# Mixture-of-experts weight loads: the sync engine's loop written out, and each load held until the third load before it has landed

## The reference, cut to what matters

```python
def expert_block(args):
    xb, e = args
    hid = jax.nn.silu(xb @ w1[e]) * (xb @ w3[e])   # w1[e], w3[e]: 1024 x 512
    return hid @ w2[e]                             # w2[e]: 512 x 1024
...
y_assign = y_slots[dest].astype(jnp.float32) * s_gate[:, None]
return jax.ops.segment_sum(y_assign, s_tok, num_segments=T)
```

## Time and profile before

| | |
|---|---|
| median of 3 runs | 3673.42 us (3670.94 to 3673.61) |
| the profiled execution: its own time | 3671.4 us |
| the profiled execution: span of its records | 3669.6 us, 29297 instructions |
| mean granted TensorE clock | 0.908 |
| PE busy / PEld busy | 81% / 43% |
| DVE / ACT / POOL busy | 18% / 13% / 7% |
| HBM traffic over the span | 160 GB/s |
| loads of `in_moe_w` | 192 of 2048 KB, median 24.4 us from issue to landing |
| writes of `y_slots` by ACT | 32 of 256 KB |

### The profile page before, as it was taken

One profiled execution on the slowest core, in us unless ns is written; L12 is line 12 of the kernel. 1 busy time (PEld: TensorE's weight loads), 2 busy tenths in 40 slices (PEclk: granted clock), 3 DMA queues, 4 the chain that ended last, 5 costly groups with the idle time before them and its releaser, 6 DMA issues. The chain is left out here.

```text
span 3669.6 us, 29297 instructions
## 1 busy us (share of the span) xinstructions
PE 2984.2 (81%) x12116; PEld 1559.9 (43%) x12116; DVE 673.6 (18%) x1777; ACT 489.9 (13%) x954; POOL 254.9 (7%) x247
## 2 busy tenths in 40 slices
PE   6999999999865455454455449999999999999999
PEld 4666666544642122122122126444444464444443
DVE  1222222210130000100100032332220123321102
ACT  1222232210010000000000021310000113110000
POOL 1000002210000000000000030020000110110000
PEclk9999999999977777787777679899999998999999
DMA  6211111112179998898889841112221211122220
GB/s 199 52 35 52 35 35 52 46 46 92 55 302 428 379 381 345 378 393 358 378 365 393 355 174 71 58 46 69 80 92 69 71 60 68 41 74 80 78 83 35
DMA packets 192664, 587.39 MB, mean 160 GB/s; under 512 B 16434, under 2 KB 142642, under 8 KB 167730
## 3 DMA queue, kind: packets, MB, share of 16 engines
q1 hardware_dynamic: 186210, 569.19, 40.3%
q10 hardware_dynamic: 4160, 8.39, 0.6%
q0 software_dynamic: 2192, 8.39, 0.6%
HBM read 571.26 MB, written 14.68 MB: 160 GB/s over the span
## 5 line engine op out<-in xcount | busy, mean ns | idle before, releaser
L2310 PE MATMUL bank<-arena 128*128 128x512 f32 (+2 forms) x1472 | 608.9, 576 | 9.1 <-DVE arena L1675 9.1
L1068 PE MATMUL bank<-arena 128*32 128x512 f32 x2048 | 264.5, 674 | 224.2 <-DMA arena<-in_moe_w 223.1
L330 PE MATMUL bank<-arena 128*128 128x384 f32 x1280 | 430.9, 489 | 14.3 <-DMA arena<-in_w_in 14.3
L2310 PEld LDWEIGHTS bank<-arena 128*128 128x128 f32 x1472 | 276.0, 191 | 340.1 <-issue 330.1
L330 PEld LDWEIGHTS bank<-arena 128*128 128x128 f32 x1280 | 237.4, 190 | 175.1 <-DMA arena<-in_w_in 14.5
L2319 PE MATMUL bank<-arena 128*128 128x512 f32 x704 | 303.2, 592 | 0.0
L1077 PE MATMUL bank<-arena 128*128 128x128 f32 x128 | 28.8, 366 | 280.6 <-DVE arena L1319 280.6
L1790 PE MATMUL bank<-arena 128*128 128x512 f32 (+3 forms) x736 | 250.2, 498 | 0.0
L1068 PEld LDWEIGHTS bank<-arena 128*32 128x32 f32 x2048 | 75.4, 122 | 411.0 <-issue 411.0
L2319 PEld LDWEIGHTS bank<-arena 128*128 128x128 f32 x704 | 133.1, 189 | 168.4 <-issue 168.4
L1790 PEld LDWEIGHTS bank<-arena 128*128 128x128 f32 x736 | 138.3, 190 | 101.2 <-issue 69.5
(11 more groups left out here) (299 smaller groups left out, 2571.7 us busy)
## 6 DMA issues: line engine op xcount, KB each, us to landing
arena<-in_moe_w SPq DMA_DIRECT2D x192, 2048.0 KB, 24.4
arena<-in_w_up SPq DMA_DIRECT2D x44, 1024.0 KB, 7.7
arena<-in_w_in SPq DMA_DIRECT2D x52, 512.0 KB, 5.7
arena<-in_w_down SPq DMA_DIRECT2D x10, 2048.0 KB, 7.7
arena<-in_w_in SPq DMA_DIRECT2D x12, 1024.0 KB, 5.2
y_slots<-arena ACTq DMA_DIRECT2D x32, 256.0 KB
arena<-in_w_in SPq DMA_DIRECT2D x4, 2048.0 KB, 9.5
arena<-in_w_out SPq DMA_DIRECT2D x4, 2048.0 KB, 8.2
```

Source lines behind the costliest of these rows:

```text
L330: ins = pe.matmul(banks[s % 2][:, 0:CW], m.aT[:, k, tile(t)], w[:, k, :], start=(k == 0), stop=(k == KT - 1))
L1068: ins = pe.matmul(banks[pr][q:q + CAP, :], m.xt[:, k, c:c + CAP], up_view(m, slots[2 * e2 + up])[:, k, :], start=(k == 0), stop=(k == KT - 1))
L2310: ins = pe.matmul(banks[2 * (j % 2) + half][:, part], w[:, k, c0:c0 + P], m.aT[:, k, part], start=(k == 0), stop=(k == KT - 1))
```

## The change

The loop is gone: the 184 loads are written out one after another, so that addresses are constants and no register is reckoned. Each load keeps its wait for a free buffer, and gets a second wait: for the landing of the load three places before it. So at most three loads are underway from the ninth load on. The first eight are issued as before.

```diff
+UNDERWAY = 3
...
-def load_expert(sp, m, G, A, at, i):
+def load_expert(sp, m, G, A, at):
 
-    pp, j = at // 6, at % 6
-    e = 8 * i + 2 * pp + (j // 2 if j < 4 else j - 4)
+    pair, j = at // 6, at % 6
+    e = 2 * pair + (j // 2 if j < 4 else j - 4)
     sp.dma_start(m.w[at % WSLOT], expert_src(A, PARTS[j], e)).then_inc(G[f"e_in{at % WSLOT}"], 16)
...
     for at in range(WSLOT):
-        load_expert(sp, m, G, A, at, 0)
+        load_expert(sp, m, G, A, at)
...
-    def loads(i, n):
-        for x in range(n):
-            pp, j = x // 6, x % 6
-            sp.wait_ge(G["up_done" if j < 4 else "down_done"], 4 * i + pp + 1)
-            load_expert(sp, m, G, A, x + WSLOT, i)
-
-    with sp.Fori(0, NIT - 1) as i:
-        loads(i, 24)
-    loads(NIT - 1, 24 - WSLOT)
+    need = Need(sp)
+    for at in range(WSLOT, NLOAD):
+        pair, j = (at - WSLOT) // 6, (at - WSLOT) % 6
+        need(G["up_done" if j < 4 else "down_done"], pair + 1)
+
+        landed = at - UNDERWAY
+        need(G[f"e_in{landed % WSLOT}"], 16 * (landed // WSLOT + 1))
+        load_expert(sp, m, G, A, at)
     sp.wait_ge(G["eb_in"], 16)
```

## The result

The changed kernel takes 3703.86 us (median of 4 runs, 3701.35 to 3708.61) against 3672.18 of the kernel before beside it: 31.7 us more, a ratio of 1.0088 with a 95% interval of 1.0071 to 1.0106. The forecast was 3674, from 3664 to 3684. The profiled execution took 3702.9 us, its span is 3701.1 us.

The account below looks back on a forecast made before the run. Two DMA engines carrying result writes beside loads were taken to bound the mixture stage; 3671.4 us profiled plus 1 for written-out code minus 0 for the wait gave 3672.4, or 3674 beside the median, range 3664 to 3684.

Parts of the forecast that it names:

- What bounds the stage: Mixture stage: two DMA engines carry all result writes besides loads and are busy throughout, 1068.1 of 1069.7 us.
- the first rival's large form: Mixture stage: a shorter load queue lets writes through and they pin no two engines; stage 947 us, total 3551, chance 0.03.
- The loop written out, priced at 1 us: SP's load issue: register work saved is worth 0; fetching more instructions costs at most 1.2 us, taken as 1.
- It bites for most loads: New landing wait in steady stretches: 5.6 loads were underway in the middle, so most issues would wait; median landing 16.8 us.
- The fourteen others only lose part of their lead: Engines without result writes: a load comes every 5.58 us and costs them 4.91, so they still end first; no cost.
- Price 0: New landing wait: the two engines' queue is refilled 8.4 us before empty, 7.0 undisturbed, so the wait costs nothing.
- The same loads in the same order: The two slow engines: both kernels give them the same loads, never dry where they weren't before; no change in time.
- the sum of 1068.1 us: Two engines' stage work: 184 loads at 4.91 us, 903.6, plus 32 writes at 5.14, 164.5; claimed to stay.
- the slower one: Rival in the mixture stage: held loads run the queue dry and 2.8 us of fixed time shows; 3682 to 3760, chance 0.11.
- its mild form: Mixture stage: the load queue runs dry at a tenth of the pairs, 9 us, giving 3682; chance 0.05.
- its full one: Mixture stage: the load queue runs dry once a pair, for 31 pairs, 87 us, giving 3760.
- some 40 us: DVE's copies in steady stretches: still 40 us apart, as each result write takes 40.4 us, with DVE waiting some 750 us.

Follow-up runs that it names:

- e5: Kernel before, with each result write issued as two, so that its slowest dimension has 64 entries and not two: 3541.79 us, ratio 0.9641.
- e1: Changed kernel without the wait for a landing, the loop still written out: 3673.54 us, ratio 0.9999 to the kernel before.
- e8: Changed kernel with each result write issued as two and two loads underway in place of three: 3541.31 us, ratio 0.9648.
- e3: Changed kernel with four loads underway in place of three: 3674.53 us, ratio 1.0006 to the kernel before.
- e4: Changed kernel with five loads underway in place of three: 3673.17 us, ratio 0.9999 to the kernel before.
- e6: Changed kernel, three loads underway, with each result write issued as two: 3541.61 us, ratio 0.9646 to the kernel before.
- e10: e6 with one more write of 2 MB per pair, on all sixteen engines, three loads underway: 3710.06 us, ratio 1.0092 to the kernel before.
- e7: Changed kernel, at most three loads underway, but issued two at a time: 3687.85 us, ratio 1.0042 to the kernel before.
- e13 to e16: Written-out loop, split result writes, plus 256 KB per pair written by SP on two engines: no landing wait 3712.10 us; three underway 3720.53, four 3712.29, two 3719.93.
- e9: e6 without the landing wait, with one more write of 2 MB per pair on all sixteen engines: 3706.90 us, ratio 1.0087 to the kernel before.

## Why the prediction was wrong

**What bounds the stage**: right, and shown. Two engines with the result writes set the pace. Spreading the writes took 131 us off, where the working of the first rival's large form (947 us of stage in place of 1070) gives 123 us and e5's own expectation 105.

**The loop written out, priced at 1 us**: right in size; e1 shows 0.1 us.

**"It bites for most loads", median landing 16.8 us, the longest under 20**: right. The page shows 17.2, and 18.2 is the longest from 1100 to 2100 us. It also bit where I said the queue would never run dry; e8 confirms that even one load ahead suffices, where the engines are even.

**"The fourteen others only lose part of their lead; a load is issued every 5.58 us and costs them 4.91, so they still end first", and with it "Price 0" for the wait**: this is the step that failed. Every number in it holds: they still end first. But I saw in it only that they don't set the pace. The same numbers say that they run out once in every load, for 0.7 us (0.6 was measured), and I took it as free because an idle engine off the path costs nothing. Shown in its place: the two engines' packets stretch by 29 us more than before (the tally), mostly in the last microsecond before the fourteen run out, only with three or fewer underway (e3, e4), and not where the engines are even and none runs empty (e6, e8, e10). The wait for the third load cost 31.7 us in place of 0.

**"The same loads in the same order", so the sum of 1068.1 us is kept**: the sum's terms, 4.91 and 5.14 us, had been read where all engines were full or where only writes ran. I carried them over to a state that the trace of before hardly has.

**The rivals**: the result has the sign of the slower one and lies between its mild form (3682 us) and its full one (3760), and PE's wait for weights rose as its sign says (223 to 241.5 us), but not by its mechanism. No queue of the two ran dry; the DMA share rose. The Trainium skill's rule that I set beside it ("DMA: Bandwidth & Descriptors", "Rules for kernel authors": issue early, wait late) would have given the right sign. Its reason, the fixed cost that should overlap, isn't what cost here: with even engines, two loads underway cost nothing. The copies' distance of "some 40 us" went to 43, and DVE's wait of 750 to 801.

**What stays open** is why the busy two slow down just before the others run out, and why a run-out costs them 0.33 us with three underway and about 0.1 with four. My theory was that the idle engines' common restart is the agent. It told right which kernels lose (those in which the fourteen run out often), but the packets contradict its mechanism: at the issues the fourteen are mostly still busy, the stretch comes before their restart, and e7 has the changed kernel's number of restarts at half its loss. And the kernel before issues into idle engines, once a pair, with two or more loads ahead on the busy two, and shows no stretch there. What the runs do show is that both an uneven load and a short queue are needed; the agent stays unnamed. e13 to e16 don't decide whether the second queue is needed too.

## What to carry to other kernels

Add up the work of each DMA engine and not only of all sixteen: a share of 0.90 can be two full engines and fourteen that wait. A transfer whose slowest dimension has few entries may be the one that pins them, and its shape is a cheap thing to change. When engines are uneven, holding loads back to few underway isn't free even if no queue runs dry (31.7 us here); look at share and GB/s together, since a rising share with a falling rate is slower packets, and then ask whose, since the engines that set the pace may have the smaller part of them. With the load evened out, the depth ceased to matter here, down to two underway. And when a theory names a moment, look at the packets around it: the restart theory fitted the times of e1, e4, e6, e7, e8 and e10, and the records show that its moment is the wrong one.

## What the runs showed of the hardware that was not expected

- The DMA engines that serve a write queue beside the loads took 6 to 7% longer for both (35.7 against 33.5 us a pair, 43.0 against 40.4 us a write) when the other fourteen ran empty at every load and three were underway. With four underway it was gone (3674.53 us). The stretched packets lie before the fourteen run out (26.8 us in the microsecond before 82 run-outs) and not after their restarts (0.7 us).
- With even engines, two loads of 2 MB underway kept the sixteen engines as full as up to seven did (3541.31 and 3541.79 us).
- A write of 2 MB more per pair on all sixteen engines (e9, 3706.90 us) cost 165 us over e5, or 5.2 us a pair: about the 5.14 us that 64 packets of 2 KB took on each of two engines when they ran alone.
